# A mixer and mixture-of-experts layer on one core: item lists written once to a DRAM table instead of made by one-hot products for every item

## The reference

```python
logits = (hf @ router_w).astype(jnp.float32) + router_b
top_logit, top_e = lax.top_k(logits, TOP_K)          # TOP_K = 4
gates = jax.nn.softmax(top_logit, axis=-1)
...
gu = xb @ w_gu[e] + b_gu[e]                          # 1024 -> 2048
g, lin = jnp.split(gu, 2, axis=-1)
g = jnp.minimum(g, 7.0); lin = jnp.clip(lin, -7.0, 7.0)
act = g * jax.nn.sigmoid(1.702 * g) * (lin + 1.0)
ys = act @ w_down[e] + b_down[e]                     # 1024 -> 1024
...
out = zeros.at[row_tok].add(ys * row_gate)           # back to the tokens, then a final rmsnorm
```

## Time and profile before

| What | Value |
|---|---|
| time, median of 3 runs | 2042.26 us (2040.45 to 2043.15) |
| span of the profiled execution | 2028.9 us |
| time of the profiled execution | not given apart; the median is 13.4 us above its span |
| PE busy in the span | 1929.8 us, 95% |
| DVE, ACT, POOL busy | 993.3, 356.2, 463.3 us |
| DMA engines, mean rate | 257 GB/s |

### The profile page before, as it was taken

The page is one execution under the profiler, slowest core; times in us unless marked ns, Lnnn a source line. Parts: engine busy times, 40 slices in busy tenths (PEclk is TensorE's granted clock), DMA queues, the critical chain, the costliest instruction groups (busy, mean ns, idle before and its releaser), DMA issues.

```text
span 2028.9 us, 54052 instructions
## 1 busy us (share of the span) xinstructions
PE 1929.8 (95%) x20292; PEld 802.2 (40%) x20293; DVE 993.3 (49%) x2301; ACT 356.2 (18%) x740; POOL 463.3 (23%) x498
## 2 busy tenths in 40 slices
PE   5999989978999899999999999999999999999996
PEld 3444434533333333334343343344433444334432
DVE  4666636355444435454454444444554455454435
ACT  4143121321110101111111111111111111111003
POOL 1210022131322222223222212222222222322221
PEclk9999999989999999999999999999999999999998
DMA  9243307341871863949595979779797797999995
GB/s 374 89 153 124 125 0 223 132 152 66 284 290 19 317 241 121 382 167 372 175 363 194 386 260 378 292 277 410 281 393 285 283 402 278 391 403 354 323 331 198
DMA packets 113439, 521.84 MB, mean 257 GB/s; under 512 B 14528, under 2 KB 32592, under 8 KB 63216
## 3 DMA queue, kind: packets, MB, share of 16 engines
q1 hardware_dynamic: 82032, 470.45, 59.1%
q0 software_dynamic: 31168, 50.78, 11.1%
q10 hardware_dynamic: 192, 0.06, 0.0%
HBM read 488.85 MB, written 32.78 MB: 257 GB/s over the span
## 4 chain that ended last, share of the span: by engine, by line
PE 85%; DMA 10%; DVE 2%; ACT 1%; issue 1%; POOL 1%; DVEq 0%; ACTq 0%; SPq 0%; POOLq 0%
PE psum L1362 42%; PE psum L1382 23%; PE psum L1095 8%; DMA big<-in_exp_w_down_dram 6%; PE psum L1269 5%; DMA big<-in_exp_w_gu_dram 3%; PE psum L1206 2%; PE psum L1138 1%; PE psum L1313 1%; PE psum L1110 0%; PE psum L1325 0%; DVE r L2114 0%; DMA big<-in_w_out_dram 0%; PE psum L1120 0%; PE psum L1224 0%
## 5 line engine op out<-in xcount | busy, mean ns | idle before, releaser
L1362 PE MATMUL psum<-big,r 128*32 128x512 f32 x9152 | 998.3, 595 | 17.3 <-DMA big<-in_exp_w_gu_dram 10.2
L1362 PEld LDWEIGHTS psum<-big,r 128*32 128x32 f32 x9152 | 291.6, 110 | 677.2 <-issue 652.9
L1382 PE MATMUL psum<-big,r 128*32 128x256 f32 x9152 | 509.9, 382 | 16.3 <-DVE r L2010 13.1
L742 POOL DMA_INDIRECT acc_rows<-r,scatter_idx x139 | 221.6, 1594 | 685.1 <-DVE r L2020 624.8
L1382 PEld LDWEIGHTS psum<-big,r 128*32 128x32 f32 x9152 | 293.7, 111 | 211.9 <-DVE r L2010 13.3
L973 ACT ACTIVATE r<-r,shift 128x128 f32<-128x128 f32 x368 | 150.9, 480 | 848.2 <-PE psum L1362 807.0
L2017 DVE TENSOR_TENSOR r<-psum,r 128x256 f32<-128x256 f32 x143 | 60.6, 424 | 268.2 <-PE psum L1382 267.2
L1995 DVE TENSOR_TENSOR r<-psum,r 128x256 f32<-128x256 f32 x143 | 60.4, 422 | 258.7 <-PE psum L1362 235.5
L1968 DVE STREAM_TRANSPOSE r<-r 128x1024 f32<-128x1024 f32 x46 | 95.9, 2086 | 170.6 <-issue 170.6
L731 POOL DMA_INDIRECT r<-hs_rows,gather_idx x143 | 142.7, 998 | 123.6 <-issue 123.6
L1095 PE MATMUL psum<-r,big 128*128 128x512 f32 x384 | 169.1, 600 | 1.6 <-ACT r L862 1.6
(11 more groups left out here) (319 smaller groups left out, 941.1 us busy)
## 6 DMA issues: line engine op xcount, KB each, us to landing
big<-in_exp_w_gu_dram SPq DMA_DIRECT2D x256, 1024.0 KB, 11.7
big<-in_exp_w_down_dram SPq DMA_DIRECT2D x128, 1024.0 KB, 16.7
big<-in_ada_w_dram SPq DMA_DIRECT2D x12, 2048.0 KB, 14.0
r<-bias_pack SPq DMA_DIRECT2D x128, 96.0 KB
r<-in_x_dram SPq DMA_DIRECT2D x16, 512.0 KB, 9.3
big<-in_w_in_dram SPq DMA_DIRECT2D x4, 2048.0 KB, 19.2
big<-in_w_out_dram SPq DMA_DIRECT2D x2, 2048.0 KB, 12.9
hs_rows<-r POOLq DMA_DIRECT2D x8, 512.0 KB, 3.1
```

The lines of the kernel that those rows point to most:

```text
L742: pool.indirect_dma_start(acc_quarters, bass.IndirectOffsetOnAxis(ap=scatter_idx[:, u:u + 1], axis=0), y_sb[:, u, :], None, bounds_check=4 ...
L1362: last = pe.matmul(psum[32 * j:32 * j + 32, u, :].rearrange("p (a n) -> p a n", a=2), izT[:, k, u * UNIT:(u + 1) * UNIT], rhs[:, :, 256 * ...
L1382: ins_ = pe.matmul(psum[32 * i:32 * i + 32, DOWN_BANK[u], 0:256], actT[:, u, f, :], down_slab(f)[:, 256 * i:256 * i + 256], start=(f == 0) ...
```

## The change

1. **The lists come from a table in DRAM.** `make_entries` on DVE works out for every one of the 4096 token and expert pairs its address in a table `lists` (the slot of its item) and its gate. POOL writes them with 32 indirect transfers of 128 rows of 8 bytes (`enter`), eight ahead of the gather of item 1 and 24 behind it. Then four plain transfers load the whole table into SBUF, and `take_lists` on DVE turns it into `quarter_of` and `gate_of`. Gathers from item 2 on wait for that (`lists_made`).
2. **One-hot products for items 0 and 1 only.** The loop loses `make_list`, `repeat_rows`, `make_onehot`, `rows_here`, `make_idx`, `make_gates` and `read_list`. The table `gate_tab` and the caps of the slots (L2023 to L2029) go too.
3. **Banks.** The down products have banks 4 to 7 to themselves. The waits for each unit become one wait ahead of the downs.
4. Some releases move: `freed[6]` to its own matmul, `freed[7]` and `freed[11]` become `gu_made` and `dn_made`.

```diff
-        DOWN_BANK = (4, 1, 2, 3)
+        DOWN_BANK = (4, 5, 6, 7)
...
+            def enter(t, j):
+                at = t * TOPK + j
+                pool.indirect_dma_start(lists, bass.IndirectOffsetOnAxis(ap=address_i[:, at:at + 1], axis=0),
+                                        entries[:, t, j, :], None).then_inc(listed, SEMW)
...
             pool.wait_ge(items_ready, 1)
-            gather(1, link)
+            pool.wait_ge(lists_blank, SEMW)
+            pool.wait_ge(tokens_entered, 1)
+            pool.wait_ge(entries_made, 1)
+            pool.wait_ge(addresses_made, 1)
+            for t in range(2):
+                for j in range(TOPK):
+                    enter(t, j)
+            gather(1, first_quarters[:, UMAX:2 * UMAX], (idx_made, 2), link)
+            for t in range(2, TT):
+                for j in range(TOPK):
+                    enter(t, j)
...
+            pool.wait_ge(listed, SEMW * TT * TOPK)
+            for i in range(4):
+                pool.dma_start(list_rows[32 * i:32 * i + 32, :, :],
+                               lists.rearrange("(b u s) w -> u b (s w)", u=32, s=UNIT)).then_inc(lists_in, SEMW)
...
-                gather(g + 2, step)
+                gather(g + 2, list_at(g + 2), (lists_made, 1), step)
...
# PE
-            make_list(2)
+            pe.wait_ge(hot_made, 2)
+            make_list(2, onehot_1, first6)
             load_word(1, 0)
             by_units(pe, units, 2, first_2a)
             repeat_rows(2)
-            make_list(3)
             load_word(1, 1)
             by_units(pe, units, 3, first_3a)
+            pe.wait_ge(gates_made, 1)
+            make_list(3, onehot, cur6, release=(freed[0], freed[1], freed[2], freed[3]))
             pe.wait_ge(z_made[1], 1)
-            repeat_rows(3, release=(freed[0], freed[1], freed[2]))
             total = item_count(pe)
             by_units(pe, units, 3, first_3b)
-            make_list(4, release=(freed[3],))
+            repeat_rows(3)
             by_units(pe, units, 2, first_2b)
-            repeat_rows(4)
             by_units(pe, units, 1, first_1b)
...
             def down_of(g):
-                make_list(g + 5, release=(freed[6], freed[7]))
+                pe.reg_add(results_before, downs, SPARE)
+                pe.wait_ge(dn_drained, results_before)
                 units_down(pe, units, down)
-                repeat_rows(g + 5, release=(freed[11],))
...
# DVE
+            def make_entries():
+                own_place = iota_e[:, :].unsqueeze(2).broadcast_to([P, NE, NE])
+                link(dve.tensor_tensor(at_expert, at_place[:, 1, :].unsqueeze(1).broadcast_to([P, NE, NE]), own_place,
+                                       ALU.is_equal))
+                link(dve.tensor_tensor(tmp, cumu, nunit, ALU.subtract))
+                link(dve.tensor_tensor(at_expert, at_expert, tmp.unsqueeze(1).broadcast_to([P, NE, NE]), ALU.mult))
+                link(dve.tensor_reduce(list_base, at_expert, AX.X, ALU.add))
+                link(dve.tensor_scalar(list_base, list_base, float(UNIT), None, ALU.mult))
+                link(dve.tensor_tensor(address, rank, list_base.unsqueeze(1).broadcast_to([P, TT, NE]), ALU.add))
+                link(dve.scalar_tensor_tensor(out=address, in0=rank, scalar=0.5, in1=address, op0=ALU.is_gt, op1=ALU.mult))
+                for t in range(TT):
+                    ins_ = dve.max(out=address8[:, t, :], in_=address[:, t, :])
+                link(ins_)
+                dve.tensor_scalar(address_i.rearrange("p (t j) -> p t j", t=TT), address8[:, :, 0:TOPK], -1.0, None, ALU.add
+                                  ).then_inc(addresses_made, 1)
+                link(dve.tensor_tensor(picked, address.unsqueeze(2).broadcast_to([P, TT, TOPK, NE]),
+                                       address8[:, :, 0:TOPK].unsqueeze(3).broadcast_to([P, TT, TOPK, NE]), ALU.is_equal))
+                link(dve.tensor_tensor(picked, picked, gate_kept.unsqueeze(2).broadcast_to([P, TT, TOPK, NE]), ALU.mult))
+                dve.tensor_reduce(entries[:, :, :, 1], picked, AX.X, ALU.add).then_inc(entries_made, 1)
+
+            def take_lists():
+                dve.wait_ge(lists_in, SEMW * 4)
+                blocks = list_rows.rearrange("p b (s w) -> p w b s", w=2)
+                link(dve.transpose(list_quarters.rearrange("p (b n) -> p b n", b=LIST_BLOCKS), blocks[:, 0, :, :]))
+                link(dve.transpose(gate_of.rearrange("p (b n) -> p b n", b=LIST_BLOCKS), blocks[:, 1, :, :]))
+                dve.tensor_scalar(quarter_of, list_quarters, quarter[:, 0:1], None, ALU.add).then_inc(lists_made, 1)
...
+            onehot_of_item_1()
+            dve.wait_ge(acc_out, SEMW * TT)
             dve.wait_ge(gates_made, 1)
-            make_onehot(1)
+            make_entries()
             read_list(2)
-            make_onehot(0)
             rows_here(2, link)
             make_idx(1, link)
-            make_gates(1, link)
             read_list(3)
-            make_onehot(2)
             rows_here(3, link)
-            make_gates(0, link)
-            read_list(4)
+            make_gates(link)
...
             units_down(dve, units, lambda u: result(u, bias_at, DOWN_BANK[u]))
+            take_lists()
             base = chain[0]
             with dve.Fori(1, last_item) as g:
...
                 block_rows(g + 1)
-                make_onehot(g + 3, step)
-                rows_here(g + 4, step)
-                make_idx(g + 2, step)
-                make_gates(g + 2, step)
                 activate_all(units, place, bias_at)
-                read_list(g + 5)
```

More of the change, by code:

```diff
@@ L168, in build @@
     acc_rows = nc.dram_tensor("acc_rows", (S + TRASH, D), F32, kind="Internal").ap()
+    lists = nc.dram_tensor("lists", (LIST_UNITS * UNIT, 2), F32, kind="Internal").ap()
     with ExitStack() as ctx:
@@ L270, in build @@
         zero = sb("zero", [P, 256])
+        blank = sb("blank", [P, 2 * P])
         ssum = sb("ssum", [P, TT])
@@ L314, in build @@
         x_in = [sem(f"x_in{t}") for t in range(TT)]
-        xr_in = [sem(f"xr_in{t}") for t in range(TT)]
         dense_in = [sem(f"dense_in{n}") for n in range(DENSE_SLOTS)]
@@ L388, in build @@
         z_blocked = sem("z_blocked")
-        freed = [sem(f"freed{q}") for q in range(CHUNKS)]
+        freed = {q: sem(f"freed{q}") for q in range(CHUNKS) if q not in (7, 11)}
         z_made = [sem(f"z_made{c}") for c in range(2)]
@@ L561, in _ @@
                 done = sp_.value_load(items_i[0:1, CUM_ITEMS + place - 1:CUM_ITEMS + place], min_val=1, max_val=MAX_ITEMS)
+                units_done = sp_.value_load(items_i[0:1, CUM_UNITS + place - 1:CUM_UNITS + place],
+                                            min_val=1, max_val=MAX_UNITS)
                 for q in range(CHUNKS):
-                    sp_.wait_ge(freed[q], done)
+                    if q == 7:
+                        sp_.wait_ge(gu_made, units_done)
+                    elif q == 11:
+                        sp_.wait_ge(dn_made, units_done)
+                    else:
+                        sp_.wait_ge(freed[q], done)
                     load_chunk(e, q)
@@ L1013, in _ @@
                 units_down(act, units, sigmoid)
-                act.wait_ge(freed[7], g + 1)
+                act.wait_ge(gu_made, through)
                 modulate(g + 1, 1)
@@ L1317, in make_list, with repeat_rows @@
                 last.then_inc(list_made, 1)
-            def repeat_rows(n, release=()):
+            def repeat_rows(n):
                 pe.wait_ge(list_read, n)
-                if not (isinstance(n, int) and n == 1):
+                if n > 1:
                     pe.wait_ge(rows_taken, n - 1)
@@ L1335, in _ @@
             downs = counter(pe, "downs")
-            results_of = [counter(pe, f"results_of{u}") for u in range(UMAX)]
-            def results_to_wait_for():
-                for u in range(UMAX):
-                    pe.reg_add(results_of[u], downs, SPARE - u)
-            results_to_wait_for()
+            results_before = counter(pe, "results_before")
             def load_word(turn, i):
@@ L1352, in begin_item, with gate_and_linear @@
                 pe.reg_add(arrived, arrived, SEMW)
-            def gate_and_linear(u, half, first=False, between=None, steady=False):
+            def gate_and_linear(u, half, first=False, between=None):
                 for k in range(4 * half, 4 * half + 4):
@@ L1364, in gate_and_linear @@
                                          start=(k == 0), stop=(k == KT - 1), skip_group_check=True)
-                    if u == 0 and k < KT - 2 and not first:
+                    if u == 0 and k < KT - 1 and not first:
                         last.then_inc(freed[k], 1)
@@ L1459, in _ @@
             signal(freed[5])
+            signal(freed[6])
             signal(gu_made)
+            pe.wait_ge(list_read, 3)
+            pe.wait_ge(rows_taken, 3)
             last_item = pe.snap(total - 1)
```

155 lines of the change are left out of this document (76 added, 79 removed).

## The result

| | before | changed |
|---|---|---|
| median | 2041.59 us (4 executions, 2040.45 to 2043.15) | 2050.55 us (4 executions, 2048.28 to 2053.61) |
| ratio | | 1.0044, 95% interval 1.0032 to 1.0056 |
| profiled execution | span 2028.9 us | span 2049.9 us, time 2051.66 us |

The page of the changed kernel (busy time by engine, then the chain's shares) against the earlier trace rows: PE does 9 us less work, as meant, and DMA's share of the chain is 13% instead of 10%.

What follows compares the result with a forecast made beforehand. Bound mostly by PE's matmuls, a tenth by weight loads. Span 2028.9 + 10 (start) - 17.4 (loop) = 2021.5, with 13.4 above the span 2035 us against a median of 2042.3; 8 in 10 range 2029 to 2049.

Steps and rivals of the forecast that it cites:

- Making the entries and the writes on POOL: At the start: DVE makes entries in 10 us, POOL writes at 1.3 us each, table loads done at 526.
- the wait for a DMA that was to be seen: Sign at the start: DVE's first table transpose near 530, after a wait for a DMA.
- writes dear: Rival at the start: each POOL write costs 1.9 us, 19 us more, time 2054; chance 0.12.
- rows land slowly: Rival at the start: 8-byte rows take twice as long, lists come some 14 us later, time 2049; chance 0.08.
- PE in the meantime: Step at the start: while POOL writes, PE starts item 1 at about 503 and ends its gate and linear part at 531.
- Ten us were forecast for the start: Cost at the start: item 2 starts at 558.2 instead of 548.23, and the 10 us go through whole.
- The wait of 11 us ahead of item 1's downs: At the start: PE waits from 531 until 542 for item 2's first activation, a wait not there before.
- The loop: Gain in the loop: 25 lists (9.8 us) and 29 repeats (8.1) saved, less 0.5 lost: 17.4 us less.
- The stretch from 1367 to 1437: In the loop: DMA engines full until 1437, PE's need 2 us later; three lists and two repeats counted as saved.
- The rival that gave the loop 12 us: Rival in the loop: only the starts' distances, 0.29 and 0.18 us, are gained; net 2, time 2040; chance 0.15.
- The time lies 13.4 above the span.: Term of the sum: the time is 13.4 us above the span, taking 2021.5 of span to 2035.

Runs made afterwards that it cites:

- a_pause6: The changed kernel with POOL waiting for landing after the 14th, 20th and 26th of its 32 writes: 2043.62 us, before 2041.89 (ratio 1.0010).
- c_best: Kernel before plus table for later items, one-hot lists kept for the first; 28 of 32 writes in turns 4 and 5, pausing after every fourth: 2037.62 us (ratio 0.9980).
- b_again: The kernel before, unchanged, run once more: 2040.71 us over ten executions, before 2040.05; profiled span 2039.2.
- b_direct: The kernel before with 32 direct writes of 128 rows of 8 bytes on POOL at the start: 2041.53 us, before 2041.89 (ratio 0.9998).
- a_direct: The changed kernel with its 32 writes direct instead of indirect, so later items work on wrong rows at the same cost: 2026.14 us, before 2041.66 (ratio 0.9915).
- b_pace4: The kernel before with 32 indirect writes of 8-byte rows at the start, POOL waiting for landing after every fourth: 2062.01 us, 20.1 more.
- b_busy: The kernel before with 32 products of 128 x 512 numbers on POOL and no added transfers: 2050.07 us, 23.2 more.

## Why the prediction was wrong, point by point

- **Making the entries and the writes on POOL: right.** 10 us forecast, 462.74 to 472.57 measured; 1.3 us a write forecast, 1.27 measured; the last write at 520.5 (forecast 520), the loads from 524 to 526.4 (forecast 526). `take_lists` took its 1.1 us, but at 540.72 instead of 530 and without the wait for a DMA that was to be seen: DVE came late from item 0's results, which is the next point. The rivals "writes dear" and "rows land slowly" did not come about: the last writes had landed 1.03 us after POOL began to wait for them. The time ended near those two rivals (2054 and 2049), but that is luck: the cause was on no list.
- **"PE in the meantime": the step that failed.** It let PE work at its own rate while POOL wrote ("item 1 starts at about 503"). It began item 1 at 539.2. Ten us were forecast for the start; measured 29.7 against an execution in the same condition, 33.5 against the trace of the prediction. With the measured terms the sum is 29.7 - 19.0 (the loop, below) = 10.7 us more instead of 7.4 less. Every write was priced on POOL and the DMA engines, and none on the engines that share nothing with POOL in the program. The experiments put 35 us on 32 indirect transfers in a row, whatever they carry, and nothing on 32 direct ones in the same place.
- **The wait of 11 us ahead of item 1's downs** did not appear, since PE was later than the lists. a_pause6 doesn't show it either, so its size stays untested. Its mechanism is real, though: in c_best DVE waits 11.47 us for the table at 717.82, and PE's down behind it is late.
- **The loop: the mechanism right, the size a little off.** An item of four units gained 0.74 us (forecast 0.67). From the wait at 604.57 to the end the changed kernel gains 12.5 us on the trace of the prediction, not 17.4. Three losses show in the trace. The first 232 products behind the wait at 604.57 took 26.78 us instead of 25.10, at a granted clock of 0.94 instead of 1.00. The stretch from 1367 to 1437, which was to end without a wait, ends with one of 1.37 us (at 1467.12 here). And three of the two-unit items' downs take 8.6 us instead of 7.11, two of them with a wait for DVE. One of these is in the last part, which brought 3.3 us (forecast 4.7): POOL gathers from 1737.40 on, DVE starts its second activation late, at 1743.42, and PE waits 0.86 us for it at 1746.54: the fault in small, as in b_again. Against b_again, which has more such downs, the gain is 19.0. The rival that gave the loop 12 us was nearer in size, but not in mechanism: 0.74 us in an item is more than its 0.47, and no hole stands at the loop's branches.
- **"The time lies 13.4 above the span."** This was the sign in plain view. All executions that list both have 1.6 to 1.9. I read the difference as launch and end, when it said that the profiled execution was 10 us faster than the usual one, and so did not show what the usual one suffers from.

## What to carry to other kernels

Before a trace is used to price a change, hold its own time against the median; if they differ by more than the change is worth, the trace lacks something that the usual execution has. Count POOL's indirect transfers in a row as a cost to PE and DVE: on this kernel 35 us for 32, so an estimate of 1.1 us each, and 9 us for 16 in the loop. In twos with pauses they made hardly a hole, but POOL was then late with its next gather; direct ones in the same place cost nothing (b_direct), though a_direct had holes that are not explained. In the traces of one set of executions there were no holes at all, so the price depends on a condition that nobody here controls. And a pause that waits for a landing is only cheap while the DMA engines are idle.

## What was not expected of the hardware

- Indirect transfers on POOL, back to back, make PE and DVE stand still (35 us for 32 of them). That it is the supply of instructions that fails is a reading, not shown: the holes have no releaser, stand inside a unit, hit PE and DVE alike, come in steps of about 0.70 us, and around a pause of POOL a run of matmuls passes, 57 in the changed kernel, mostly 59 to 64 in b_pace4 and 65 to 93 in a_pause6. The Trainium skill ("Runtime: NRT & Kernel Launch", Instruction fetch mechanics) says that each engine's sequencer fetches its code in blocks of 256 instructions through its own DMA queue while it executes. With their weight loads the runs of matmuls here are some 114 to 186 instructions, fewer than a block, and no run shows a fetch that is late.
- The same kernel in the same environment has two conditions, 2041 and 2027 us, in whole sets of executions. In the faster one the three traces have no hole. What makes it is open, and the changed kernel was not run in it.
- POOL's products slow DVE. In b_busy the two-input product of DVE takes 1.47 us instead of 0.43 and a clamp up to 1.40 instead of 0.28, while the sums that read PSUM keep their 0.42:

```profile
499.19 0.42 DVE L1999 SCALAR_TENSOR_TENSOR r<-psum,r 128x256 f32<-128x256 f32 x1
...
499.72 1.40 DVE L2005 TENSOR_SCALAR r<-r 128x256 f32<-128x256 f32 x1
501.15 1.47 DVE L2008 TENSOR_TENSOR r<-r 128x256 f32<-128x256 f32 x1
```

The Trainium skill ("SBUF — State Buffer", SBUF: two separate sides) describes a pair of ports that DVE and POOL lock against each other for a whole instruction; by that rule the wait is as long as what is left of POOL's product, and the trace agrees: 1.47 is about what one product of POOL takes there (45.81 us for 32 is 1.43 each).
